# Root and spatial sums spread through HBM, running sums on the vector engine, in a two-layer encoder

## The reference

```python
h = rms_norm(x, norm_mix_g[i])
if i % 2 == 0:
    p = h @ w_in_even[e]                       # 2048 x 3072
    z = gelu(p[..., :2048])                    # u and v
    y_a = spatial_gating(z, ln_g, ln_b, w_spatial, b_spatial)
    y_b = multiscale_pool(p[..., 2048:], w_pool, scale)
    mix = concatenate([y_a, y_b]) @ w_out_even[e]
else:
    p = h @ w_in_odd[o]                        # q, k, v and 16 forget columns
    log_f = log_sigmoid(p[..., 6144:] + b_forget)
    c = cumsum(log_f, axis=1)                  # over the 256 tokens, per head
    logits = q @ k.T * scale + c[q] - c[k]     # causal
    mix = (softmax(logits) @ v) @ w_out_odd[o]
x = x + mix
x = x + conv_ffn(rms_norm(x, norm_ffn_g[i]), w_up, conv_w, conv_b, w_down)

# spatial gating, per group g of 4: w is w_spatial where block_causal_mask allows it
v = group_layer_norm(v, ln_g, ln_b)
gate = einsum('gts,bnsgd->bntgd', w, v) + b_s
return u * gate
```

## Time and profile before

| | |
|---|---|
| median of 3 runs | 2106.95 us (2106.84 to 2107.01) |
| profiled execution | 2106.81 us, span of the core 2105.0 us |
| PE busy | 2094.1 us, 99% of the span |
| DVE, ACT, POOL busy | 1452.3, 1044.5, 29.4 us |
| DMA | 397.18 MB, mean 189 GB/s |

### The profile page before, as it was taken

The page is one execution under the profiler, slowest core; times in us unless marked ns, Lnnn a source line. Parts: engine busy times, 40 slices in busy tenths (PEclk is TensorE's granted clock), DMA queues, the critical chain, the costliest instruction groups (busy, mean ns, idle before and its releaser), DMA issues.

```text
span 2105.0 us, 29641 instructions
## 1 busy us (share of the span) xinstructions
PE 2094.1 (99%) x11082; PEld 1808.6 (86%) x11082; DVE 1452.3 (69%) x1596; ACT 1044.5 (50%) x1078; POOL 29.4 (1%) x59
## 2 busy tenths in 40 slices
PE   9999999999999999999999999999999999999998
PEld 7888888888888888888888888888888888888886
DVE  6785586777677776776556555576776767767677
ACT  7554454445444454455444444454444444544454
POOL 0000000000000000000001000000000000000000
PEclk9999999999999999999999999999999999999999
DMA  8655466555555655554665555555655556555552
GB/s 297 202 174 204 141 219 200 181 198 184 194 191 185 203 179 188 197 196 155 196 188 176 187 173 185 184 180 184 209 182 180 199 180 204 193 180 195 184 193 107
DMA packets 317299, 397.18 MB, mean 189 GB/s; under 512 B 8724, under 2 KB 240956, under 8 KB 317116
## 3 DMA queue, kind: packets, MB, share of 16 engines
q1 hardware_dynamic: 313500, 391.27, 55.9%
q0 software_dynamic: 1056, 3.16, 0.8%
q10 hardware_dynamic: 2688, 1.99, 0.3%
HBM read 394.29 MB, written 2.11 MB: 188 GB/s over the span
## 4 chain that ended last, share of the span: by engine, by line
PE 99%; DVE 0%; ACT 0%; issue 0%; POOL 0%; DVEq 0%; ACTq 0%; POOLq 0%
PE ps_turned L1315 39%; PE ps_straight L1354 36%; PE ps_turned L1324 20%; PE ps_turned L1386 1%; PE ps_straight L1609 0%; PE ps_straight L1626 0%; PE ps_straight L1618 0%; PE ps_straight L1418 0%; PE ps_straight L1487 0%; PE ps_straight L1636 0%; PE ps_turned L1565 0%; PE ps_turned L1560 0%; PE ps_straight L1561 0%; PE ps_straight L1560 0%; PE ps_turned L1561 0%; PE ps_straight L1565 0%
## 5 line engine op out<-in xcount | busy, mean ns | idle before, releaser
L839 DVE TENSOR_TENSOR w_low<-w_raw,w_high 128x2048 fp32r<-128x2048 f32 x369 | 846.4, 2295 | 431.2 <-ACT w_high L456 383.3
L456 ACT ACTIVATE w_high<-w_raw 128x2048 fp32r<-128x2048 f32 x368 | 705.0, 1918 | 684.4 <-PE ps_straight L1354 307.9
L1315 PE MATMUL ps_turned<-h_split,w_high 128*128 128x512 f32 x3584 | 832.3, 390 | 0.0
L1315 PEld LDWEIGHTS ps_turned<-h_split,w_high 128*128 128x128 f32 x3584 | 667.6, 188 | 135.3
L1324 PEld LDWEIGHTS ps_turned<-h_split,w_low 128*128 128x128 f32 x3584 | 440.7, 192 | 6.1 <-issue 0.2
L1324 PE MATMUL ps_turned<-h_split,w_low 128*128 128x256 f32 x3584 | 445.3, 283 | 0.0
L1354 PE MATMUL ps_straight<-w_high,y_split 128*128 128x512 f32 x1856 | 441.1, 390 | 0.0
L1354 PEld LDWEIGHTS ps_straight<-w_high,y_split 128*128 128x128 f32 x1856 | 347.5, 188 | 71.6
L1354 PE MATMUL ps_straight<-w_low,y_split 128*128 128x512 f32 x928 | 229.2, 389 | 0.0
L1354 PEld LDWEIGHTS ps_straight<-w_low,y_split 128*128 128x128 f32 x928 | 174.2, 188 | 36.2
L1058 DVE SCALAR_TENSOR_TENSOR work<-work,conv_columns 128x256 f32<-128x256 f32 x352 | 154.5, 480 | 10.9
(11 more groups left out here) (201 smaller groups left out, 604.5 us busy)
## 6 DMA issues: line engine op xcount, KB each, us to landing
w_raw<-in_w_up SPq DMA_DIRECT2D x176, 1024.0 KB, 5.0
w_raw<-in_w_down SPq DMA_DIRECT2D x88, 1024.0 KB, 5.0
w_raw<-in_w_in_odd SPq DMA_DIRECT2D x48, 1024.0 KB, 5.2
w_raw<-in_w_in_even SPq DMA_DIRECT2D x23, 1024.0 KB, 5.3
w_raw<-in_w_out_even SPq DMA_DIRECT2D x16, 1024.0 KB, 5.0
w_raw<-in_w_out_odd SPq DMA_DIRECT2D x16, 1024.0 KB, 5.0
work<-c_rows POOLq DMA_DIRECT2D x8, 256.0 KB, 4.6
x<-in_x SPq DMA_DIRECT2D x3, 512.0 KB, 10.9
```

What stands on the lines that cost most here:

```text
L456: a.activation(wh[:, s, :], raw[:, s, :], ACT.Copy).then_inc(s_high, 1)
L839: ve.tensor_tensor(wl[:, s, :], raw[:, s, :], wh[:, s, :].bitcast(F32), ALU.subtract).then_inc(s_low, 1)
L1315: ins = pe.matmul(psT[:, 2 * slot + m, :], hi[:, kk, P * m:P * m + P], acts[:, K, :], start=(K == 0 and not narrow_ran), stop=(K == KC - 1 ...
```

## The change

Three paths are laid in another way.

1. **Root.** DVE stops at the root itself (s_rcol). POOL's `spread_rstd` stores its two columns into row 0 of `c_dram`, 256 elements of 4 bytes, waits for the landing (s_rst) and loads the row into all partitions of rstdT (s_rstd). `diag`, the products and the copy go. `take_rstd` is only a wait, in an FFN at k == 2 instead of k == 1, in the first stage at n == 8 instead of n == 5.
2. **Spatial sums.** DVE reduces w_sp along the free dimension (the unmasked part, two reductions), POOL stores four columns of 128 elements and loads 256 KB into WTsum. The product and the copy go.
3. **Forget gate.** The forget weights stand in 48 columns (high, high, low), so the parts come out on partitions that DVE can add; ACT copies two parts of 16x256; the logits stay in rows, 16 heads x 256 tokens, and the running sum is one `tensor_tensor_scan` along the free dimension. PE turns the result in two small pieces at k == 5 (`turn_sums`) where `cumulate` stood at k == 4. `tri` goes, and cneg is taken from the sums.

```diff
+            def spread_rstd(s):
+                pool.wait_ge(s_rcol, s + 1)
+                pool.dma_start(c_dram[0:1, :].rearrange("o (t p) -> p (o t)", p=P), rstd,
+                               allow_slow_non_contiguous=True).then_inc(s_rst, 16)
+                pool.wait_ge(s_rst, 16 * (s + 1))
+                pool.dma_start(rstdT[:, :], c_dram[0:1, :].to_broadcast([P, TOK])).then_inc(s_rstd, 16)
+            spread_rstd(0)
+            pool.wait_ge(s_wsum, 1)
+            for g in range(AG):
+                pool.dma_start(c_dram[1 + g // 2:2 + g // 2, P * (g % 2):P * (g % 2) + P].rearrange("o p -> p o"),
+                               wsum[:, g:g + 1],
+                               allow_slow_non_contiguous=True).then_inc(s_wsd, 16)
+            pool.wait_ge(s_wsd, 16 * AG)
+            pool.dma_start(WTsum.rearrange("p g t -> p (g t)"),
+                           c_dram[1:3, :].rearrange("r n -> (r n)").unsqueeze(0).to_broadcast([P, AG * P])).then_inc(s_wsb, 16)
+            spread_rstd(1)
...
             bias_tile(0)
             with pool.Fori(0, HEADS // 2 - 1) as r:
                 bias_tile(1, r)
+            spread_rstd(3)
...
                     if first == 0 and k == 2:
                         a.wait_ge(s_f, 1)
-                        fenced(a.activation(fT, psA[0:2 * HEADS, 2, :], ACT.Copy), s_fT, 1)
+                        a.activation(f_xl, psA[0:HEADS, 2, TOK:], ACT.Copy).then_inc(s_fT, 1)
+                        fenced(a.activation(f_wl, psA[2 * HEADS:3 * HEADS, 2, 0:TOK], ACT.Copy), s_fT, 2)
...
             def spread_rstd(s):
 
                 ve.wait_ge(s_sd, s + 1)
-                refined_rsqrt(rstd, ms, sd, rr, nt)
-                for t in range(2):
-                    ins = ve.tensor_scalar(diag[:, t, :], ident[:, :], rstd[:, t:t + 1], None, ALU.mult)
-                fenced(ins, s_diag, s + 1)
+                refined_rsqrt(rstd, ms, sd, rr, nt, last=s_rcol, count=s + 1)
 
             def take_rstd(s):
-                ve.wait_ge(s_bc, s + 1)
-                bank = psA[:, 3, :] if s else psT[:, 1, :]
-                fenced(ve.tensor_copy(rstdT[:, :], bank[:, 0:TOK]), s_rstd, s + 1)
+                ve.wait_ge(s_rstd, 16 * (s + 1))
...
+                ve.tensor_reduce(wsum[0:64, :], w_sp[0:64, :, 0:64], AX_X, ALU.add)
+                fenced(ve.tensor_reduce(wsum[64:P, :], w_sp[64:P, :, :], AX_X, ALU.add), s_wsum, 1)
...
-                    if k == 1:
+                    if k == 2:
                         take_rstd(s)
...
+                        take_rstd(2)
+                        ve.wait_ge(s_fT, 2)
+                        link(ve.tensor_tensor(fl, psA[0:HEADS, 2, 0:TOK], f_xl, ALU.add))
+                        link(ve.tensor_tensor(fl, fl, f_wl, ALU.add))
+                        link(ve.tensor_tensor(fl, fl, rstdT[0:HEADS, :], ALU.mult))
+                        link(ve.tensor_scalar(fl, fl, bf, None, ALU.add))
...
-                        fenced(ve.scalar_tensor_tensor(out=lf, in0=fl, scalar=0.0, in1=fe, op0=ALU.min, op1=ALU.subtract),
-                               s_lf, 1)
-                    if first == 0 and k == 4:
+                        fenced(ve.tensor_tensor_scan(sums, fl, fe, 0.0, ALU.add, ALU.subtract), s_lf, 1)
+                    if first == 0 and k == 5:
                         ve.wait_ge(s_c, 1)
                         link(ve.tensor_copy(cq, psA[:, 2, 0:32].rearrange("p (t h) -> p t h", t=2)))
-                        fenced(ve.tensor_scalar(cneg, psA[0:HEADS, 3, 0:TOK], -1.0, None, ALU.mult), s_cq, 1)
+                        fenced(ve.tensor_scalar(cneg, sums, -1.0, None, ALU.mult), s_cq, 1)
```

More of the change, by code:

```diff
@@ L122, in build @@
         rstdT = sb("rstd_rows", [P, TOK])
-        diag = sb("diag", [P, 2, P])
         small = sb("small", [P, 160])
@@ L135, in build @@
         inv_count = small[:, 120:136]
-        both_parts = small[0:2 * HEADS, 136:136 + HEADS]
+        wsum = small[:, 152:156]
         spare = work[:, 3584:4096].rearrange("p (m t) -> p m t", m=2)
@@ L157, in build @@
         probsT = work[:, 3072:3456]
-        bf = work[:, 3456:3472]
+        bf = work[0:HEADS, 3456:3457]
         bias = work[:, 4096:4864].rearrange("p (h k) -> p h k", h=2)
-        fT = work[0:2 * HEADS, 4096:4608]
+        f_wl = work[0:HEADS, 2064:2320]
+        fl = work[0:HEADS, 2320:2576]
+        fe = work[0:HEADS, 2576:2832]
+        f_xl = work[0:HEADS, 4864:5120]
+        sums = work[0:HEADS, 4480:4736]
         cneg = work[0:HEADS, 4096:4352]
@@ L164, in build @@
         q_rstdT = work[:, 5248:5504]
-        tri = work[:, 5504:5632]
-        fl, fe, lf = (work[:, 5632 + 32 * i:5664 + 32 * i].rearrange("p (t h) -> p t h", t=2) for i in range(3))
         final_g = work[:, 0:2048]
@@ L682, in ffn @@
                             .then_inc(s_wf, 16)
-                        a.dma_start(bf, b_forget.to_broadcast([P, HEADS])).then_inc(s_wf, 16)
+                        a.dma_start(bf, b_forget.rearrange("o h -> h o"), allow_slow_non_contiguous=True).then_inc(s_wf, 16)
                     if l == 0 and k == 10:
                         a.wait_ge(s_wf, 32)
-                        fenced(a.activation(wf_split[:, :, 0:HEADS], wf_raw.rearrange("p (k h) -> p k h", k=KC), ACT.Copy),
-                               s_wfs, 1)
+                        twice = wf_raw.rearrange("p (k h) -> p k h", k=KC).unsqueeze(2).to_broadcast([P, KC, 2, HEADS])
+                        fenced(a.activation(wf_split[:, :, 0:2 * HEADS].rearrange("p k (i h) -> p k i h", i=2), twice,
+                                            ACT.Copy), s_wfs, 1)
                     if k in (2, 4, 6, 8):
@@ L1003, in _ @@
                 if n == 8:
+                    take_rstd(0)
+                    ve.wait_ge(s_wsb, 16)
                     ve.wait_ge(s_z, 2)
@@ L1138, in ffn @@
                         ve.wait_ge(s_wfs, 1)
[L1139 removed]
+                        fenced(ve.tensor_tensor(wf_split[:, :, 2 * HEADS:], wf_raw.rearrange("p (k h) -> p k h", k=KC),
                                                 wf_split[:, :, 0:HEADS].bitcast(F32), ALU.subtract), s_wfs, 2)
[L1141 to L1142 removed]
                     if k == 5:
@@ L1388, in transpose_x @@
                 ins.then_inc(s_turn, 1)
-            def spread(s):
-                pe.wait_ge(s_diag, s + 1)
-                bank = psA[:, 3, :] if s else psT[:, 1, :]
-                for t in range(2):
-                    ins = pe.matmul(bank[:, P * t:P * t + P], ones[:, :], diag[:, t, :], start=(t == 0), stop=True,
-                                    skip_group_check=True)
-                ins.then_inc(s_bc, 1)
             def warm(count):
@@ L1458, in _ @@
                         ins.then_inc(s_spT, 1)
-                    if n == 4:
-                        spread(0)
-                    if n == 6:
-                        pe.wait_ge(s_WT, 1)
-                        pe.matmul(psT[:, 0, :], ones[:, :], WT.rearrange("p g t -> p (g t)"), start=True, stop=True)\
-                            .then_inc(s_wsum, 1)
-            pe.wait_ge(s_wsr, 1)
+            pe.wait_ge(s_WT, 1)
             for j in range(4):
@@ L1575, in ffn @@
                 turned_half(B + 2, 1, 0, H)
-                spread(s)
                 turned_half(B + 3, 1, 1, H)
@@ L1690, in heads_of_group @@
                         forget_sums()
-                        spread(2)
-                    if first == 0 and k == 2:
-                        turn_forget_sums()
-                    if first == 0 and k == 4:
-                        cumulate()
+                    if first == 0 and k == 5:
+                        turn_sums()
                     if first and k in (0, 2, 4):
```

77 lines of the change are left out of this document (23 added, 54 removed).

## The result

The changed kernel takes 2128.75 us (median of 5 runs, 2126.53 to 2129.66) against 2106.84 for the kernel before (2106.41 to 2107.01): a ratio of 1.0103, with a 95% interval of 1.0092 to 1.0114. It is slower by 21.9 us, where 5 us less were forecast. The profiled execution of the changed kernel has a span of 2127.4 us.

What follows compares the result with a forecast made beforehand. PE was taken to bound the kernel: 5.33 us of work removed less 0.3 added gives 5.0 off, round trips hidden at cost 0, so 2106.81 - 5.0 = 2101.8 (2101.9 on the median); range 2101.0 to 2104.5.

Steps and rivals of the forecast that it cites:

- What bounds the kernel: Whole run: PE, busy 2094.1 of 2105.0 us; removed products shorten it, late answers cost nothing until PE runs dry.
- Work off PE: PE's stream: 5.33 us of products and stretch removed, 0.3 added for two turns, net 5.0 us.
- The root's round trip, FFN: Each FFN: POOL's store and load bring rstdT 6.5 (up to 7.7) us after the root; cost 0.
- a cover of 9.9 us: Each FFN, before panel 2: rstdT may come until 9.9 us after the root before PE lacks its PSUM slot.
- the store's landing: Root's store of 256 elements of 4 bytes: taken to land in 2.4 us, with 6.0 as the upper end.
- First stage: Root early; spatial sums through HBM arrive at 63.5 against DVE's step at 64.21; cost 0.
- The root leads by far: First stage: root's chain row is at 40.36, its first use on DVE behind 64.21.
- DVE runs three pieces ahead of PE: 0: First stage: DVE's work behind the sums' wait runs over 15 us ahead of PE, so lateness costs 0.
- The forget stage: Heads: log of the gate about 1 us later, hidden by k == 5; bias at 1027.2, cover 5.7; cost 0.
- A late root, large: Rival, PE before panel 2 of either FFN: store takes twice 6.0, 6.2 us per FFN, 2114.3 us; chance 0.06.
- The descriptors: Rival, POOL's DMA issues wait for DVE's work: round trip 11.1, 1.2 us over in both FFNs, 2104.3; chance 0.04.
- the small one: Rival of a slightly late root: round trip 11.3 against 9.9, PE stands 1.4 us per FFN, 2104.7; chance 0.11.

Runs made afterwards that it cites:

- after_row: Changed kernel, computed in full: columns copied into one SBUF row and stored as one piece, DVE's waits moved to the first instruction needing the rows; 2102.03 us, ratio 0.9977.
- after_wide: Changed kernel with 4-byte store pieces replaced by as many 512-byte pieces, root's rows and spatial sums left out of the computation; 2102.44 us, ratio 0.9979.
- after_pitch: Changed kernel with the same 4-byte store pieces laid 64 bytes apart, root's rows and spatial sums left out of the computation; 2102.38 us, ratio 0.9978.
- sums_only: Kernel before with only the spatial sums sent through HBM, root and forget gate as before; 2108.69 us, ratio 1.0011.
- forget_only: Kernel before with only the forget gate's running sums moved to DVE, root and spatial sums as before; 2104.64 us, ratio 0.9988.
- probe2: Kernel before with the forget gate's part alone, plus 30 single POOL DMAs, ten forms three times, each some 22 us after the one before; 2104.76 us.
- probe: Kernel before with the forget gate's part alone, plus 30 POOL DMAs in the first FFN, one right behind the other, of small and wide pieces; 2104.66 us.

## Why the prediction was wrong

Step by step, in its own order.

- **What bounds the kernel: right.** An answer that comes late costs nothing until PE has run dry, and then it costs all of the rest, and the lower clock on top.
- **Work off PE: right.** Net 5.0 were forecast; before minus after_row is 4.85 in time, before minus after_wide 4.6. The chain gives 1.22 in the first stage, or 1.37 counted from PE's first turn of x (forecast 1.30), 0.45 and 0.44 in the FFNs (0.44 each) and 2.63 in the heads (2.85). The added turns cost 0.22 and 0.26 of stretch behind, 0.48 for the 0.3 taken; that accounts for most of the rest. The forget product with 48 columns took 3.71 us where it took 3.70 with 32, so that 0 was right.
- **The root's round trip, FFN: wrong, and this is the step that failed.** The frame held: a cover of 9.9 us, and PE stops where it was said. The term was the store's landing: 2.4 taken, 6.0 as its upper end, 8.7 to 10.1 measured. The load was 3.8 taken, 5.0 at most, 6.5 to 7.3 measured. A part of this is its own mis-sizing: with quick stores it is 5.9 and 5.3 (medians of after_wide and after_pitch). That the rest comes from the weights held up before it, which move beside it at 300 GB/s and more, is a reading of the trace. From the root to the add it is 17.2, and 17.2 - 9.9 = 7.3 stands against the 7.09 that PE waited.
  The choice itself was the fault. The c_rows store (16 pieces of 1 KB) was taken as nearest "in engine, direction and bytes", and the 128 KB load in 2048 pieces of 64 B as proof that many pieces are quick. Neither has pieces of 4 B beside each other in memory, and no row of before has; the bound from b_forget (6.0) was a bound of rows, not of the operation. after_wide and after_pitch show that the store's estimate was near for two other layouts (2.2 and 2.0, both below the 2.4 that the prediction held to be the least).
- **What was not in the sum at all:** that the store stops the loads behind it (27 for 300 GB/s), and that PE comes out of a stall at a lower granted clock (1.8 and 2.4 us). Each FFN lost 9 us with a stall of 7.
- **First stage: wrong.** "The root leads by far" held for the root, but the sums were forecast at 63.5 and came at 70.4 (landing 11.45 for 2.4 to 6.0), and "DVE runs three pieces ahead of PE: 0" did not hold: DVE had work for 97% of its time up to the piece that PE then missed, so 3.6 us of lateness cost 2.4 (sums_only), and with the root's store beside it 6.97.
- **The forget stage: right where it stands alone** (forget_only: -2.4, forecast 2.41). The scan of 256 columns took 0.68 for the 0.5 taken. In the change it waits 8.6 us for the root's rows, which the step "the root is loaded while PE does the forget sums" had as hidden; PE then waits 1.2, and the heads lose 1.79.
- **The rivals.** "A late root, large" named the place, the direction and the trigger, and got 0.06. Its price, 6.2 us per FFN and 2114.3 in all, fits the stalls alone (7.09 and 6.66); the rest to 2128.8 is the clock, the loads and the first stage. The descriptors were no matter: POOL's issues of the two round trips took 0.54 to 0.86 each. The 10.5 ns a packet of the Trainium skill ("DMA: Bandwidth & Descriptors", "Measured (HBM→SBUF, 128 partitions, SWDGE, issued from GpSimd)"), by which the store "would still meet the 9.9 us", gave an estimate of 2.7 for a landing of 9.1; that table is of loads.
- **The chances.** A chance of 0.73 for faster rested on one unseen operation, with 3.4 us of cover between gain and loss. What was known was that no row showed it; the range's end should have been what the rivals' prices gave, not half of the small one.

Two rules of the Trainium skill can be set beside this. "DMA: Bandwidth & Descriptors", "Specifications", puts the least transfer for full rate at 512 B, since below it the DMA engine reads, modifies and writes. Here 128 pieces of 4 B at a pitch of 16 B land as early as 128 of 512 B, so falling below that size is not what costs here; touching small pieces is. The same page of the Trainium skill, "Back-pressure in remote DMA", says of copies between cores that stalled writes stall the source engine's other queues too; the 27 GB/s during the store look like that within one core. Whether the slow pieces wait for each other's read, modify and write of one place is a guess that fits and that no run here settles.

## What to carry to other kernels

Price a DMA by the layout of its pieces in memory, and not by its bytes or by another DMA of the same queue: where no row of the profile has that layout, measure it in the kernel before anything depends on it. Before a column goes to memory, turn it into a row in SBUF. Put the wait on a transfer at the first instruction that reads what it brings, behind every add or copy that frees a bank for PE. Ask of the engine behind the wait how busy it is: one with no gaps carries a lateness on to the end of the stage. And add up a late answer as three prices: the wait, the lower clock behind it, and what the slow transfer does to the loads beside it.

## What was unexpected of the hardware

- Stores of touching 4-byte pieces to memory: 64 to 256 of them took 8.4 to 12.6 us, 32 took 6.2, 16 took 4.9; 16 bytes apart, 128 of them took 4.8 like everything else.
- Loads issued behind such a store nearly stop (27 GB/s at a DMA share of 0.18, 300 GB/s without it), those under way before it do not (367 GB/s in probe2), and a 128 KB load issued next takes 6.5 to 7.3 us, with quick stores 5.3 to 5.9 (medians).
- Reading such pieces is not slow: loads of 256 touching pieces of 4 B landed after 4.5 us (probe, median).
- A copy of 128 x 4 B from 128 partitions into one row of SBUF is quick: 1.9 and 2.3 us (medians) in after_row, with touching pieces in the destination.
- PE's granted clock fell from 1.00 to 0.50 while PE stood for 7 us, and was at 1.00 again from 286, 4 us after PE went on; the next 32 wide products took 9.09 us instead of 7.28.
